# Seven fast-product groups in the first MLP, GpSimd adds half of a norm's squares, and late squares get places of their own

## The reference

```
# block 1, second half
x = x + relu(rms_norm(x, norm_mlp) @ w1)**2 @ w2     # w1: 1024 x 4096, w2: 4096 x 1024
x = x * rsqrt(mean(x*x) + eps) * norm_final          # the end norm of block 1
# block 2
u = rms_norm(x, norm1_g_2)                           # a second norm right behind it
z = u @ w_in_2                                       # queries, keys, values of a retention mixer ...
h = x + mixer(u) ; h = h + relu(rms_norm(h) @ w_up)**2 @ w_down ; out = rms_norm(h)
```

## Time and profile before

| what | us |
|---|---|
| median of 3 runs | 2302.3 |
| the profiled execution | 2303.79 |
| its span | 2302.0 |
| TensorE (PE) busy | 2282.0 (99%) |
| VectorE (DVE) busy | 1595.3 (69%) |
| GpSimd (POOL) busy | 1116.4 (48%) |
| ScalarE (ACT) busy | 815.5 (35%) |
| granted TensorE clock, mean | 0.997 |

### The profile page before, as it was taken

One profiled execution on the slowest core, in us unless ns is written; L12 is line 12 of the kernel. 1 busy time (PEld: TensorE's weight loads), 2 busy tenths in 40 slices (PEclk: granted clock), 3 DMA queues, 4 the chain that ended last, 5 costly groups with the idle time before them and its releaser, 6 DMA issues.

```text
span 2302.0 us, 32329 instructions
## 1 busy us (share of the span) xinstructions
PE 2282.0 (99%) x10840; PEld 1901.4 (83%) x10840; DVE 1595.3 (69%) x2247; ACT 815.5 (35%) x1330; POOL 1116.4 (48%) x1256
## 2 busy tenths in 40 slices
PE   8999999999999999999999999999999999999998
PEld 6888888888888888888888888888888888888886
DVE  6666666756787778776666666545687877787766
ACT  4233333324544434443430002002363444344432
POOL 4322222344566566655543333444556665666561
PEclk9999999999999999999999999999999999999999
DMA  4101010124254555455312111111235545554553
GB/s 146 46 28 37 28 36 28 37 73 144 94 197 148 186 182 198 146 185 183 110 55 73 37 37 37 46 47 46 100 138 183 187 146 195 182 187 146 196 194 136
DMA packets 56966, 264.87 MB, mean 115 GB/s; under 512 B 6960, under 2 KB 8112, under 8 KB 39600
## 3 DMA queue, kind: packets, MB, share of 16 engines
q1 hardware_dynamic: 55872, 262.10, 33.5%
q10 hardware_dynamic: 1008, 1.62, 0.2%
HBM read 206.03 MB, written 57.67 MB: 115 GB/s over the span
## 4 chain that ended last, share of the span: by engine, by line
PE 94%; DVE 3%; DVEq 1%; ACT 1%; DMA 0%; issue 0%; SPq 0%; POOL 0%; ACTq 0%; POOLq 0%
PE prod_ps L719 13%; PE prod_ps L721 13%; PE prod_ps L720 13%; PE prod_ps L978 8%; PE prod_ps L976 8%; PE prod_ps L977 8%; PE side_ps L978 7%; PE side_ps L977 7%; PE side_ps L976 7%; PE side_ps L856 2%; PE side_ps L772 2%; PE side_ps L778 2%; PE side_ps L786 1%; PE side_ps L796 1%; PE side_ps L788 1%; PE prod_ps L1010 1%
## 5 line engine op out<-in xcount | busy, mean ns | idle before, releaser
L719 PE MATMUL prod_ps<-operand_hi,w_hi 128*128 128x512 f32 x1336 | 533.3, 399 | 3.4 <-DVE hgrn_v_t L1397 1.6
L721 PE MATMUL prod_ps<-operand_hi,w_lo 128*128 128x512 f32 x1336 | 522.3, 391 | 0.0
L720 PE MATMUL prod_ps<-operand_lo,w_hi 128*128 128x512 f32 x1336 | 521.3, 390 | 0.0
L556 POOL CAST w_hi<-w_raw 128x1024 fp32r<-128x1024 f32 x82 | 87.7, 1069 | 669.7 <-PE prod_ps L721 645.2
L560 POOL TENSOR_TENSOR w_lo<-w_raw,w_hi 128x256 fp32r<-128x256 f32 x328 | 313.2, 985 | 6.6
L719 PEld LDWEIGHTS prod_ps<-operand_hi,w_hi 128*128 128x128 f32 x1336 | 251.6, 188 | 56.5 <-POOL w_lo L686 2.8
L721 PEld LDWEIGHTS prod_ps<-operand_hi,w_lo 128*128 128x128 f32 x1336 | 251.2, 188 | 53.8
L720 PEld LDWEIGHTS prod_ps<-operand_lo,w_hi 128*128 128x128 f32 x1336 | 251.8, 188 | 48.4
L590 POOL TENSOR_TENSOR w_lo<-w_raw,w_hi 128x256 fp32r<-128x256 f32 x168 | 155.6, 944 | 130.5 <-ACT w_hi L2486 130.3
L590 POOL TENSOR_TENSOR w_lo<-w_s,w_hi 128x256 fp32r<-128x256 f32 x168 | 129.2, 772 | 143.5 <-ACT w_more_hi L2494 115.8
L1816 DVE TENSOR_TENSOR x_res<-prod_ps,x_res 128x512 f32<-128x512 f32 x130 | 89.0, 685 | 98.4 <-PE prod_ps L978 98.4
(11 more groups left out here) (365 smaller groups left out, 5416.9 us busy)
## 6 DMA issues: line engine op xcount, KB each, us to landing
w_raw<-stream SPq DMA_DIRECT2D x202, 512.0 KB, 3.7
x_park<-x_res SPq DMA_DIRECT2D x45, 1024.0 KB, 7.9
x_res<-x_park SPq DMA_DIRECT2D x45, 1024.0 KB, 6.8
swapped<-op_park SPq DMA_DIRECT2D x39, 1024.0 KB, 5.2
op_park<-swapped SPq DMA_DIRECT2D x6, 1024.0 KB, 7.3
x_in<-x_t SPq DMA_DIRECT2D x16, 256.0 KB, 5.4
x_res<-x_t SPq DMA_DIRECT2D x8, 512.0 KB, 4.6
out_t<-x_res SPq DMA_DIRECT2D x16, 256.0 KB, 2.1
```

What stands on the lines that cost most here:

```text
L556: nc.gpsimd.tensor_copy(w_hi[:, slot], w_raw[:, slot]).then_inc(high_made, 1)
L719: nc.tensor.matmul(into, w_h, a_h, start=(k == 0), stop=False)
L720: nc.tensor.matmul(into, w_h, a_l, start=False, stop=False)
L721: last = nc.tensor.matmul(into, w_l, a_h, start=False, stop=(k == KT - 1))
```

## The change

1. `GROUPS` becomes (7, 7). The first MLP has seven groups, and its plain down product has four hidden tiles, through the same `last_down` as the second MLP, with the half tiles in the order of tiles (`TILE_ORDER`). The code for the two up products behind the last group goes. The weight units are laid out anew: four fewer plain units and four more units in pairs; four empty units keep the numbering, are never loaded, and are counted on by GpSimd.
2. In `last_down`, for both MLPs, the first four half tiles end in another order: the first two end before the third and fourth take their last two hidden tiles.
3. GpSimd adds the gained squares of half 1 (`add_gained`, eight instructions of 128x512), which ACT now writes into `sig`. It does this between the splits of the last weight units.
4. For the last six half tiles (numbers 10 to 15) ACT writes its squares into places of their own, and DVE adds these nine pieces behind all low parts (`add_late`). `norm_sum` goes up once before the last piece and once after it.
5. TensorE makes both pairs of sums together, behind the first unit's second half; for the second pair it also waits for GpSimd's eight additions.

```diff
-GROUPS = (6, 7)
+GROUPS = (7, 7)
...
+        LATE_PIECES = tuple((n, gained) for n in range(10, 2 * KT) for gained in range(2 - n % 2))
...
 # GpSimd, behind the last group of the first MLP
+                def add_gained(m):
+                    pool.wait_ge(sq_ready, 32 + 4 * m + 4)
+                    if m:
+                        pool.wait_ge(gained_added, m)
+                    nc.gpsimd.tensor_tensor(sq_sum_g[:, 1], sq_sum_g[:, 1], sig[:, m % 2], ALU.add
+                                            ).then_inc(gained_added, 1)
+                add_gained(0)
+                split_unit(down + 2, 0, (prod, 2 * down + 4))
+                add_gained(1)
+                add_gained(2)
+                split_unit(down + 3, 1, (prod, 2 * down + 8))
...
+                add_gained(3)
+                add_gained(4)
+                split_unit(U_IN2, 0, (prod, 2 * down + 12))
+                for m in range(5, KT):
+                    add_gained(m)
+                split_unit(U_IN2 + 1, 1)
...
 # TensorE
-                for n in range(4):
+                for n in range(2):
                     piece(n, (2,), h_count)
-                for n in range(4):
+                for n in range(2):
                     piece(n, (3,), h_count).then_inc(prod, 1)
+                for n in range(2, 4):
+                    piece(n, (2, 3), h_count).then_inc(prod, 1)
...
-                up_pair(groups, 2, 3, 4, near_banks)
-                up_pair(groups, 3, 5, 6, far_banks)
...
+                last_down(u, h_count, LAST_ORDER if index else TILE_ORDER)
...
                 product(u, s0, 0, 0, count, mid=old("v"))
+                if not first:
+                    ret_old(n - 1, "kv")
+                product(u, s0, 1, 0, count)
                 if first:
                     both_sums(0)
+                    both_sums(1)
...
 # DVE
+                def add_late(piece, gained):
+                    half = piece % 2
+                    dve.wait_ge(sq_ready, sq_before + 2 * piece + gained + 1)
+                    total = sq_sum_g if gained else sq_sum
+                    nc.vector.tensor_tensor(total[:, half], total[:, half], late_home(piece, gained), ALU.add)
...
 # ACT
+                            if half and m >= 2:
+                                act.wait_ge(gained_added, m - 1)
+                            into = sig[:, m % 2] if half else late_home(n, 1) if late else work[:, slot + 1]
```

More of the change, by code:

```diff
@@ L406, in half_chunks @@
             return range(half * NB // 2, (half + 1) * NB // 2)
+        TILE_ORDER = [(m, half) for m in range(KT) for half in range(NH)]
         LAST_ORDER = [(m, half) for m in range(KT - 4) for half in range(NH)]
@@ L522, in mlp @@
                 group(groups - 1)
-                for n in range(2 if index else -2, 4 if index else 2):
+                for n in range(2, 4):
                     load_next(u0 + down + n, n % 2)
                 for n in range(len(SWAPPED)):
-                    if index:
-                        fetch_behind(groups - 1, 3, 10, n)
-                    else:
-                        fetch_behind(groups, 3, 6, n)
+                    fetch_behind(groups - 1, 3, 10, n)
             for k in range(KT):
@@ L673, in split_mlp @@
                         split_unit(down + j, j % 2, (prod, 2 * down + 4 * (j - 1)))
+                    return
+                def add_gained(m):
[9 more added lines that the diff above has]
+                split_unit(down + 3, 1, (prod, 2 * down + 8))
+                pool.wait_ge(w_split, down + PAIRS)
+                pool.sem_inc(w_split, PAIRS)
+                pool.sem_inc(high_made, PAIRS)
+                for slot in range(2):
+                    pool.sem_inc(w_landed[slot], 16 * PAIRS // 2)
+                add_gained(3)
[4 more added lines that the diff above has]
+                split_unit(U_IN2 + 1, 1)
             for u in range(2):
@@ L996, in end_spread, with last_down @@
                 spread(t % 2, chunks=half_chunks(half))
-            def last_down(u, h_count):
+            def last_down(u, h_count, order):
                 def piece(n, ks, count=None):
-                    m, half = LAST_ORDER[n]
+                    m, half = order[n]
                     act = slice(half * HALF, (half + 1) * HALF)
@@ L1031, in last_down @@
                 piece(1, (0, 1), h_count)
-                for n in range(4):
+                for n in range(2):
                     piece(n, (2,), h_count)
-                for n in range(4):
+                for n in range(2):
                     piece(n, (3,), h_count).then_inc(prod, 1)
+                for n in range(2, 4):
+                    piece(n, (2, 3), h_count).then_inc(prod, 1)
                 for n in range(4, 13):
                     whole(n)
+                if order is not LAST_ORDER:
+                    for n in range(13, 16):
+                        whole(n)
+                    return
                 end_sums(0)
@@ L1298, in ret_iteration @@
                 product(u, s0, 0, 0, count, mid=old("v"))
+                if not first:
+                    ret_old(n - 1, "kv")
+                product(u, s0, 1, 0, count)
                 if first:
                     both_sums(0)
+                    both_sums(1)
                 else:
-                    ret_old(n - 1, "kv")
-                product(u, s0, 1, 0, count, mid=(lambda: both_sums(1)) if first else None)
-                if not first:
                     ret_old(n - 1, "o")
@@ L1683, in advance @@
                             finish(*divmod(2 * m + half - 1, 2))
+                finish(KT - 1, 1)
                 if with_gain:
-                    dve.drain()
-                    dve.sem_inc(norm_sum, 1)
-                finish(KT - 1, 1, with_gain)
+                    for n, (piece, gained) in enumerate(LATE_PIECES):
+                        if gained == 0 and piece % 2 == 0 and n:
+                            dve.drain()
+                        if piece == 2 * KT - 1 and gained == 0:
+                            dve.drain()
+                            dve.sem_inc(norm_sum, 1)
+                        add_late(piece, gained)
                 dve.drain()
@@ L2581, in squares_early, with squares_late @@
                             then(n)
-                def squares_late(g, r, u, h, b, then=None, between=None, behind=None, later=None):
+                def squares_late(g, r, u, h, b, then=None, between=None, behind=None):
                     act.wait_ge(evac, at(g, 16, 2 * (u0 + u) + 2))
@@ L2909, in mlp_units @@
             units += up_pair(tile + 2)
-        if index:
-            return units + [upper_unit(w2, groups * WINO_K, 2 * p * P) for p in range(PAIRS)]
-        units += up_pair(FF // P - 4) + up_pair(FF // P - 2)
-        return units + [unit(w2, groups * WINO_K, m * P) for m in range(KT)]
+        return units + [upper_unit(w2, groups * WINO_K, 2 * p * P) for p in range(PAIRS)]
     blocks = [unit(*block) for block in blocks]
     blocks += mlp_units(a["mlp_w1"][0], a["mlp_w2"][0], 0)
+    blocks += [np.zeros((P, KT, P), np.float32)] * (KT - PAIRS)
     after_mlp = len(blocks)
```

124 lines of the change are left out of this document (41 added, 83 removed).

## The result

The changed kernel took 2307.04 us (median of 19 runs, 2305.53 to 2309.32), the kernel before 2302.62 in the same comparison (19 runs, 2301.58 to 2304.22): ratio 1.0018, 95% interval 1.0012 to 1.0024. It is slower by some 4.4 us, where 2302.0 was forecast with 2306.0 as the upper end. The profiled execution took 2308.49 us, its span 2306.7, its mean clock 0.994 (0.997 before).

What follows compares the result with a forecast made beforehand. TensorE, busy 2282.0 of 2302.0 us, was taken to bound the kernel. Matmuls saved -5.85, wait +4.0 and slower clock +1.5 gave -0.35 us: 2302.0 us from a median of 2302.3, range 2296.6 to 2306.

Steps and rivals of the forecast that it cites:

- What goes: First MLP's down product: 24 matmuls fewer, 5.44 us; with most of a 0.5 us wait and its restart, 5.85 us saved.
- GpSimd's 128x512 addition: Gained-square additions on GpSimd: 1.26 us each, holding the port shared with DVE for some 1.14 us.
- the layout: DVE's and GpSimd's instructions around the first MLP's end, laid one behind the other by their durations to time the late sum.
- The wait: TensorE's one-column sums behind the first MLP wait for DVE's late norm_sum, delayed by GpSimd on the shared port: 4.0 us.
- T + 15: First norm_sum 15 us after T, the end of the last down matmul; TensorE reaches its sums at T + 10.9.
- The clock: Behind the wait at the sums, TensorE's clock falls to half and costs 1.5 us, with 0 and 3 as ends.
- the sums at 36.5 us: Earlier place in the trace: short waits, then granted clock 0.55 and 0.60 over 38 to 42 us, costing 1.7 us.
- rival (b): The wait at the sums comes but the clock holds: 2300.4 us; chance 0.14.
- The sum: Whole kernel: -5.85 + 4.0 + 1.5 = -0.35 us, giving 2302.0 us on the median.
- (c): Slower: GpSimd ahead of DVE nearly every time, sum 9.7 us late, clock falls: +5.3, 2307.6 us; chance 0.09.
- the 10.5 from which (c) was to decide: TensorE's loss above which the slower rival decides: 5.85 saved plus 4.6, the limit of no change.

Runs made afterwards that it cites:

- 13: Changed kernel with VectorE making all square additions, reordered by halves, GpSimd's third-unit split held, second sums behind six matmuls of the next unit: 2296.93 us.
- 3: Changed kernel with GpSimd's split of the next stage's third unit held until VectorE's last norm_sum: 2306.21 us.
- 10: Changed kernel with only the second set of sums moved behind six matmuls of the next unit, the spread nine matmuls later: 2307.05 us.
- 9: Kernel before with only both sets of sums put in a row behind the product of the first unit's second half: 2305.30 us.
- 5: Changed kernel with three of GpSimd's casts made by ScalarE and the next stage's second- and third-unit splits held: 2307.13 us.
- 2: Changed kernel without GpSimd's eight additions and the waits for them, sums still in a row: 2298.81 us.
- 1: Changed kernel with 18 unread 128x512 products on TensorE ahead of its wait for norm_sum: 2304.70 us.
- 7: Changed kernel without GpSimd's eight additions, second set of sums moved behind six matmuls of the next unit: 2297.21 us.
- 8: Changed kernel with three casts on ScalarE, third-unit split held, VectorE's last additions reordered, six matmuls between the sets of sums: 2304.46 us.
- 11: Changed kernel with third-unit split held, VectorE's nine last additions reordered by halves, second sums behind six matmuls of the next unit: 2303.12 us.
- 6: Changed kernel with VectorE making all additions of squares, GpSimd's eight gone, sums still in a row: 2301.69 us.
- 12: Changed kernel with third-unit split held, last additions reordered, sums set apart, and two of GpSimd's casts on ScalarE: 2303.75 us.

## Why the prediction was wrong

- **What goes: right.** -5.85 forecast, -5.83 in the changed kernel, -5.88 in 13.
- **GpSimd's 128x512 addition: right.** 1.26 forecast, 1.30 to 1.32 measured alone; VectorE's addition beside it 1.78, the 0.57 + 1.14 and the overlap of the layout.
- **The wait: right, 4.0 forecast, 4.3 measured**, with `norm_sum` at T + 15 and T + 15.2. That it is so near is partly luck. The third unit's cast at 1223.85 was missing in the layout, and with that split held back the wait is 1.6 us shorter (3): the instructions that were in the layout come to 2.5 us.
- **The clock: wrong, the step that failed.** "Here part of it falls on the sums, which are not set by the clock alone; I take 1.5, with 0 and 3 as ends." It measured 5.0: 2.6 on the sums, 2.4 on the twelve matmuls behind. The size was taken, as its working says, from the sums at 36.5 us, where the clock was below full for the 4 us from 38 to 42; here it was at half for 10.2 us. Two things in the rows were misread. The sums do go with the clock, 1.70 us becoming 3.4 for the second set of the changed kernel (1228.58 to 1231.99) and for the first in 10, so they cost as the products do. And the change's own fifth part was counted as free but for its cover: that the two sets at 1222 and 1227 left the clock at full was noted, for rival (b), without asking what parts them. In the kernel before it was wide products, and the change takes these away. By itself that costs 1.7 us by the medians and 2.9 in the trace (9). The place at 36.5 us could have told: TensorE was idle for 0.26 us from 36 to 38 and 0.8 from 32 to 34, short waits indeed, and the clock fell behind sixteen sums with no wide product among them.
- **The sum.** -5.83 + 4.30 + 5.0 = +3.5; the stretch says +3.32. With 4.0 and 5.0 in place of 4.0 and 1.5 the forecast would have been 2305.5: a loss in place of a small gain, but still within the range and 1.5 under the median of 2307.0. What carries the time past 2306 is some 1.1 us more between the stretch and the medians, and these stay unassigned; in other runs they differ by as much in either direction (9: +2.93 and +1.74).
- **Rivals.** (c), the slower one, came nearest in time (2307.6) by another way: VectorE was 4.3 us late, not 9.7, and the clock brought the loss to 9.3. That is under the 10.5 from which (c) was to decide, so the change stays just within 0.2%, but above the range.
- **What stays open** is how the clock's loss in one execution divides between wait and row: each does it alone (10, and 5 ahead of wide products; 2 and 9). The one trace with both has 10.2 us of half clock, the one with the wait alone 17, and their medians are the same, so the costs of the two don't add up.

The Trainium skill, "TensorE: Matmul & The Clock Gate", section "Why this matters for your kernels", gives idle gaps between bursts of matmuls as what brings the clock back to half. Runs 5 and 10 agree, with gaps of 4.6 and 4.2 us. Runs 2 and 9 go beyond it: TensorE was busy 4.00 of 4.00 and 3.00 of 3.00 us, with one-column products, and its clock was at 0.50 behind them. Here the measurement decides: it fell without a gap.

## What to carry to other kernels

Put one-column products between wide ones; thirty-two in a row cost 1.8 to 3.5 us in the traces here (2, 9, 1), and with six wide matmuls between two sets of sixteen, and no wait, the clock stayed up (7, 13). A wait of more than 4 us that a change added cost 2 to 3 us beyond its length inside the MLP (5, 8) and, ahead of the sums, 7 in one trace and some 5 by the medians (10); one of 1.6 us cost more than its length in some executions only (11): look at the spread of the runs, not at one profile. And work handed from VectorE to GpSimd was no help here, where both read SBUF: eight additions of 0.6 us there cost VectorE more than they saved (6).

## What the runs showed of the hardware

Useless products in place of a wait made this kernel faster (1: 1.6 us in the stretch, 2.3 in the medians).

VectorE and GpSimd do not always take turns, as the layout of the prediction had it. In 12, GpSimd's four subtractions that follow ScalarE's cast, and then VectorE's timeline beside them:

```profile
1196.25 6.40 POOL L569 TENSOR_TENSOR w_lo<-w_raw,w_hi 128x256 fp32r<-128x256 f32 x4 [4.68 <-ACT w_hi L2521]
```
```profile
1196.38 0.68 DVE L1436 TENSOR_TENSOR sq_sum<-sq_sum,work 128x512 f32<-128x512 f32 x1
1196.98 0.68 DVE L1715 TENSOR_TENSOR x_res<-prod_ps,x_res 128x512 f32<-128x512 f32 x1
1197.58 0.74 DVE L1440 SCALAR_TENSOR_TENSOR operand_lo<-x_res,gain,operand_hi 128x512 fp32r<-128x512 f32 x1
1198.24 0.68 DVE L1436 TENSOR_TENSOR sq_sum<-sq_sum,work 128x512 f32<-128x512 f32 x1
1198.84 0.68 DVE L1436 TENSOR_TENSOR sq_sum_g<-sq_sum_g,work 128x512 f32<-128x512 f32 x1
```

Here VectorE runs at its full pace of 0.60 to 0.66 and GpSimd needs 6.40 us for what took 4.04 in turns and 2.82 alone: as far as the rows tell, the residual additions (line 1715), which read PSUM, are the gaps in which GpSimd gets through. The Trainium skill, "SBUF — State Buffer", section "SBUF: two separate sides", says that whichever starts first holds the shared pair for its whole instruction. The trace of the changed kernel agrees (VectorE's addition takes 1.78 us beside GpSimd's of 1.32), and the one of 12 adds that VectorE, whose instructions follow without a gap, kept it there. Why they took turns in the one place and not in the other was not tried.
